# An order of its own for each engine in a recurrence over pairs of heads, with the loop written out

## The chip, the cores and the metric

The kernel runs on one core of a Trainium2 chip. The time is the device time of one execution in microseconds (us); three runs were timed. One further execution was recorded by the hardware profiler. The engines are named as in its rows: PE is the matmul engine (PEld its weight loads, PEq its instruction sequencer), DVE the vector engine, ACT the activation engine, POOL and SP the two that issue most transfers here.

## The reference, cut to what matters

A prompt of 256 tokens and 8 decode sequences of 4 tokens go through two layers of width 2048. The first layer's mixer is RWKV-7: projections r, k, v, a decay w, a rate a, and for each of 32 heads of size 64 a state matrix S that is stepped over the tokens:

```
def _wkv_step(S, inp):
    r_t, w_t, k_t, v_t, a_t, b_t = inp
    Sa = jnp.einsum('bhvk,bhk->bhv', S, a_t)
    S = S * w_t[:, :, None, :] + Sa[..., None] * b_t[:, :, None, :] + v_t[..., None] * k_t[:, :, None, :]
    y = jnp.einsum('bhvk,bhk->bhv', S, r_t)
    return S, y
...
S_last, ys = lax.scan(_wkv_step, wkv_prev.astype(f32), xs)
...
y = ((y - ym) * lax.rsqrt(yv + GN_EPS)).reshape(B, T, D) * gn_g.astype(f32) + gn_b.astype(f32)
bonus = jnp.sum(r_h * k_h * r_k.astype(f32), axis=-1, keepdims=True) * v_h
y = (y + bonus.reshape(B, T, D)).astype(x.dtype)
out = (y * g) @ w_o
```

After it come DeepNorm layer norms, SwiGLU feed-forward layers and, in the second layer, a pooling mixer. Outputs are the new tokens and the new states.

## The kernel before

All activations lie in SBUF with features on the partitions and the 288 tokens along the free axis. Every dense product is three matmuls on two halves of each operand (high times high, high times low, low times high): ACT makes the high half of a weight slab, DVE the low half, PE multiplies. The engines run their own instruction streams, in order, and meet at semaphores; `Steps` gives each engine a counter for each pair, and `await_step` waits for a named step.

The change lies in the stage of the recurrence, between the projections r, w, a, g and the product with `rw_g2`. It works on pairs of heads (128 rows): 16 pairs `p`, of which the even ones use the tiles and the three PSUM banks of `pairs[0]`, the odd ones those of `pairs[1]`. The recurrence is done in chunks of 64 tokens. The work on one pair is cut into three parts, each a Python generator whose `yield` ends a phase; each engine has its own generator, with its own instructions in the same phases:

- DENSE, phases D0 to D10: k, v and the small products for w and a of a pair. The weights come in nine pieces of 256 KB (`fetch`, three slots); PE multiplies a piece in each of D0 to D3 and D6 to D9 (D4 w, D5 a, D7 also the norm of k). DVE makes the low halves (`piece_lo`, L1607), in D9 also a reciprocal; ACT makes the high halves, in D4 k, kk and sq, in D5 the sigmoid sg, in D6 a, in D8 root, in D10 v.
- FRONT, F0 to F10: DVE's scan of the decays (L1672), csx, feats; PE turns the decode state (s0), then tok, prod (F3), two (F4), and three levels of a block inverse, x0 t0 x1 t1 x2 t2 (F5 to F10). DVE answers prod with "two" and the masks (F3), each x with a masked copy, each t with a sum (L1737), t2 also with uvx (L1748). ACT copies what PE leaves in PSUM: s0t, tok (F2), two (F4), wr, qt.
- BACK, B0 to B12: the last two levels x3 t3 x4 t4 (B0 to B3), q (B4), s0c (B5), and for the chunks 1 to 3 u and s (B6 to B11), y (B12). DVE updates the decode state in B1 (L1752, L1755), makes bonv (B4), st0 (B5, L1765), u and st, and stores y (B12, L1787). ACT copies the decode state to SOS (B2), makes mv (B3), q (B4), sop (B12).

The group norm of a pair's y is done while the next pair of the same tiles is in FRONT: PE makes the mean (L747) in F0 and the variance (L750) in F1; DVE centres in F0 and does the rest in F4 (reciprocal L1637, three more operations to L1640); ACT squares in F0 and takes the root in F2. For the last pairs this is a part of its own, NORM (N0 to N4).

`weave` puts the phases of two or three parts into one order by a fixed fraction, the same on all engines: with all three, F0 D0 B0 F1 D1 B1 B2 F2 D2 B3 F3 D3 B4 F4 D4 B5 F5 D5 B6 F6 D6 B7 B8 F7 D7 B9 F8 D8 B10 F9 D9 B11 F10 D10 B12. I call one such call a weave: in it one pair is in BACK, the next in FRONT and the one after in DENSE. `turns` makes 18 of them: the first has no BACK, the second no norm yet, twelve stand in a loop of six iterations (`Fori`, L376), the thirteenth is written out behind it, one has no DENSE, and two end with NORM. On PE a wait on a loop's index needs a register, which `await_step` computes (L732).

POOL stores the decode states of a pair when SOS is there and then loads those of the next pair of the same tiles (`results`, `states`). Scans (L1672) mark the weaves in the trace: each weave but the last two begins with one.

Of the kernel before, what the change touches and what calls it, by code (L numbers as in the profile page):

```python
# [115 lines left out]
def build(nc, x_prompt, x_sample, state_wkv, state_shift, state_pool, ln_g, ln_b, rw_mu, rw_wr, rw_wk, rw_wv,  # L116
# [4 lines left out]
    with ctx:  # L121
# [78 lines left out]
        pairs = []  # L200
# [158 lines left out]
        FRONT, BACK, NORM, DENSE = 0, 1, 2, 3  # L359
        LEVELS = [range(3), range(3, 5)]  # L360
        PHASES = [11, 13, 5, 11]

        def weave(program, *parts):


            at = [((n + (0.8 if part[2] == BACK else 0.5)) / PHASES[part[2]], q) for q, part in enumerate(parts) for n in range(PHASES[part[2]])]
            running = [program(pairs[b], 2 * i + b, i, part, normed[0] if normed else None) for b, i, part, *normed in parts]
            for _, q in sorted(at):
                next(running[q])
            assert all(next(q, None) is None for q in running)  # L370

        def turns(eng, program):
            last = KC // 2 - 1
            weave(program, (0, 0, FRONT), (1, 0, DENSE))
            weave(program, (0, 0, BACK), (1, 0, FRONT), (0, 1, DENSE))
            with eng.Fori(0, last - 1) as i:  # L376
                weave(program, (1, i, BACK), (0, i + 1, FRONT, i), (1, i + 1, DENSE))
                weave(program, (0, i + 1, BACK), (1, i + 1, FRONT, i), (0, i + 2, DENSE))
            weave(program, (1, last - 1, BACK), (0, last, FRONT, last - 1), (1, last, DENSE))
            weave(program, (0, last, BACK), (1, last, FRONT, last - 1))  # L380
            weave(program, (1, last, BACK), (0, last, NORM, last))
            weave(program, (1, last, NORM, last))

        MIXED = 6 * KC

# [246 lines left out]
        def _(pe):  # L632
# [367 lines left out]

            pe.wait_ge(lhl_ready, 4)
            pe.wait_ge(out_free, 4 + len(FIRST))
            weave(pair, (0, 0, DENSE))
            pe.wait_ge(wkv_const, 16)
            turns(pe, pair)
            for z in pairs:
                pe.wait_ge(z.ndve.sem, z.ndve.value("done", KC // 2 - 1))
            pe.sem_inc(wkv_done, 1)
# [128 lines left out]
        def _(act):  # L1137
# [243 lines left out]
            act.wait_ge(wkv_const, 16)  # L1381
            act.wait_ge(xkept, 16)

            turns(act, pair)
            for z in pairs:
                act.wait_ge(z.ndve.sem, z.ndve.value("done", KC // 2 - 1))
            act.wait_ge(wkv_done, 3)
# [86 lines left out]
            for j in range(4):  # L1474
                q = SLAB["pool"] // 4 + (j + 2) // 4
                hi(q, (j + 2) % 4, SLAB["pool"] + j + 2)
                for m in range(4):
                    n = 4 * j + m
# [10 lines left out]
        def _(dve):  # L1489
# [319 lines left out]
                next(begun)  # L1809
            dve.wait_ge(wkv_const, 16)  # L1810

            turns(dve, pair)
            for z in pairs:
                dve.wait_ge(z.ndve.sem, z.ndve.value("done", KC // 2 - 1))
            dve.sem_inc(wkv_done, 1)
# [131 lines left out]
            for lv in range(4):  # L1947
                d, f = 1 << lv, 4 * lv
                a, b = lv % 2, (lv + 1) % 2
# [26 lines left out]
            for j in range(4):  # L1976
                lo(SLAB["pool"] + j + 2, (j + 2) % 4)
                for m in range(4):
                    n = 4 * j + m
# [39 lines left out]
```

## Time and profile before

| | us |
|---|---|
| three runs | 3199.43 median, 3194.06 to 3199.57 |
| profiled execution, its own time | 3202.89 |
| its span, first to last instruction | 3201.2 |
| PE busy | 2834.5 (89%) |
| DVE busy | 1587.4 (50%) |
| ACT busy | 1193.3 (37%) |
| granted PE clock, mean | 0.932 of full |

Busy time is the union of an engine's instructions. Matmuls are pipelined and their ends modelled, so a busy PE may still be at half clock; the clock column of a stretch tells. 1.00 is 2.4 GHz and 0.50 is 1.2 GHz; values between are stretches that hold both. The recurrence runs from 254.55 us (the first scan) to 1143 us.

### The profile page before, as it was taken

To read this page: it belongs to the slowest core of one execution; us is meant where nothing else is said; L and a number is where in the kernel's file an instruction comes from. 1 tells how busy PE (TensorE), PEld (TensorE's weight loads), DVE (VectorE), ACT (ScalarE), POOL (GpSimd) and SP (SyncE) were. 2 spreads that over 40 slices of the span, in tenths; PEclk is the share of its full clock that TensorE was granted. 3 is DMA by queue.
4 is the path that set the end of the run, shared out by engine and by line. 5 is a ranking of instruction groups with operands and counts; after the bars stand their busy time and mean duration, and the time that the engine had idled before them with its cause. 6 is when DMAs were issued, how large, how long until landed. Compare 5 with 4: busy or idle time off the path is not lost.

```text
span 3201.2 us, 61665 instructions
## 1 busy us (share of the span) xinstructions
PE 2834.5 (89%) x24731; PEld 2669.6 (83%) x24731; DVE 1587.4 (50%) x2341; ACT 1193.3 (37%) x1618; POOL 170.9 (5%) x247
## 2 busy tenths in 40 slices
PE   5868888888888859899999999995699999999997
PEld 4867767667777649799999999994699999999996
DVE  5565655556555444544444444446544444444444
ACT  4344433333333122444423333334444423333333
POOL 0000010110101001000000000002100000000001
PEclk9888998889989779899999999997799999999998
DMA  6422121111212046356556565452255546665452
GB/s 189 116 54 74 54 53 53 47 54 50 53 48 56 9 138 169 98 165 170 149 145 182 166 167 161 135 169 81 66 162 166 166 135 170 174 168 166 134 162 66
DMA packets 703974, 379.37 MB, mean 119 GB/s; under 512 B 15159, under 2 KB 696487, under 8 KB 703383
## 3 DMA queue, kind: packets, MB, share of 16 engines
q1 hardware_dynamic: 697632, 361.35, 40.3%
q0 software_dynamic: 6128, 15.45, 2.0%
q8 instruction: 122, 2.00, 0.3%
q10 hardware_dynamic: 70, 0.39, 0.0%
q14 instruction: 22, 0.18, 0.0%
HBM read 367.33 MB, written 10.62 MB: 118 GB/s over the span
## 4 chain that ended last, share of the span: by engine, by line
PE 80%; DVE 11%; issue 3%; ACT 3%; DMA 1%; POOL 1%; PEld 1%; DVEq 1%; SPq 0%; PEldq 0%; ACTq 0%; POOLq 0%
PE PS L635 22%; PE PS L636 22%; PE PS L637 21%; PE PS L812 4%; DVE WL L1493 2%; ACT WH L1142 1%; PE PS L1030 1%; PE PS L864 1%; DVE TM L1637 1%; PE PS L900 1%; DVE PL L1607 1%; DVE ML L1507 1%; DVE TM L1501 1%; PE PS L836 1%; PE PS L936 1%
## 5 line engine op out<-in xcount | busy, mean ns | idle before, releaser
L1493 DVE TENSOR_TENSOR WL<-RAW,WH 128x2048 fp32r<-128x2048 f32 (+1 forms) x346 | 706.4, 2043 | 888.1 <-ACT WH L1142 888.0
L635 PE MATMUL PS<-MH,WH 128*128 128x288 f32 x3456 | 1028.6, 298 | 97.7 <-DVE ML L1507 36.3
L636 PE MATMUL PS<-ML,WH 128*128 128x288 f32 x3456 | 1031.8, 299 | 0.0
L637 PE MATMUL PS<-MH,WL 128*128 128x288 f32 x3456 | 1030.6, 298 | 0.0
L1142 ACT ACTIVATE WH<-RAW 128x2048 fp32r<-128x2048 f32 (+1 forms) x346 | 593.2, 1715 | 969.3 <-PE PS L637 947.8
L635 PEld LDWEIGHTS PS<-MH,WH 128*128 128x128 f32 x3456 | 661.3, 191 | 101.9 <-issue 71.4
L636 PEld LDWEIGHTS PS<-ML,WH 128*128 128x128 f32 x3456 | 660.9, 191 | 0.0
L637 PEld LDWEIGHTS PS<-MH,WL 128*128 128x128 f32 x3456 | 659.9, 191 | 0.0
L635 PE MATMUL PS<-HH,WH 128*128 128x288 f32 x1408 | 417.3, 296 | 16.4 <-DVEq L1893 16.4
L636 PE MATMUL PS<-HL,WH 128*128 128x288 f32 x1408 | 419.0, 298 | 0.0
L637 PE MATMUL PS<-HH,WL 128*128 128x288 f32 x1408 | 418.5, 297 | 0.0
L635 PEld LDWEIGHTS PS<-HH,WH 128*128 128x128 f32 x1408 | 268.4, 191 | 17.3 <-DVEq L1893 17.3
L636 PEld LDWEIGHTS PS<-HL,WH 128*128 128x128 f32 x1408 | 268.3, 191 | 0.0
L637 PEld LDWEIGHTS PS<-HH,WL 128*128 128x128 f32 x1408 | 268.0, 190 | 0.0
L635 PE MATMUL PS<-MH,PH 128*128 128x288 f32 x512 | 183.4, 358 | 12.9 <-DVE PL L1607 12.9
L636 PE MATMUL PS<-ML,PH 128*128 128x288 f32 x512 | 167.1, 326 | 0.0
L637 PE MATMUL PS<-MH,PL 128*128 128x288 f32 x512 | 165.6, 324 | 0.0
L1607 DVE TENSOR_TENSOR PL<-PR,PH 128x512 fp32r<-128x512 f32 x144 | 94.6, 657 | 126.0 <-ACT PH L1230 123.9
L635 PEld LDWEIGHTS PS<-MH,PH 128*128 128x128 f32 x512 | 112.0, 219 | 24.2 <-issue 12.9
L1436 ACT ACTIVATE HH<-TM 128x288 f32 (+1 forms) x88 | 39.1, 445 | 234.2 <-DVE TM L1890 234.2
L636 PEld LDWEIGHTS PS<-ML,PH 128*128 128x128 f32 x512 | 112.5, 220 | 0.7
L637 PEld LDWEIGHTS PS<-MH,PL 128*128 128x128 f32 x512 | 111.7, 218 | 0.0
(268 smaller groups left out, 2926.4 us busy)
## 6 DMA issues: line engine op xcount, KB each, us to landing
RAW<-in_ffn_w_in SPq DMA_DIRECT2D x176, 1024.0 KB, 5.7
RAW<-in_ffn_w_down SPq DMA_DIRECT2D x128, 704.0 KB, 4.7
RAW<-in_rw_wr SPq DMA_DIRECT2D x16, 1024.0 KB, 5.9
PR<-in_rw_wk SPq DMA_DIRECT2D x64, 256.0 KB, 2.8
PR<-in_rw_wv SPq DMA_DIRECT2D x64, 256.0 KB, 2.8
RAW<-in_rw_wo SPq DMA_DIRECT2D x16, 1024.0 KB, 6.0
RAW<-in_rw_g SPq DMA_DIRECT2D x4, 1024.0 KB, 5.9
S0N<-in_state_wkv POOLq DMA_DIRECT2D x64, 64.0 KB, 2.5
```

The lines of the kernel that those rows point to most:

```text
L635: pe.matmul(out, wh, xh, start=first, stop=False)
L636: pe.matmul(out, wh, xl, start=False, stop=False)
L637: return pe.matmul(out, wl, xh, start=False, stop=last)
L812: ins = pe.matmul(bank[hr[r], col + u * CH:col + (u + 1) * CH], lhs(hr[r], u), rhs(hr[r], u), start=True, stop=True)
L836: pe.transpose((PA, PB)[t][:, n * P:(n + 1) * P], f[:, t * P:(t + 1) * P], IDN)
L864: ins = pe.matmul(bank[:, t * 256:(t + 1) * 256], z.KF[hr[h], t * P:(t + 1) * P], z.AR[hr[h], :, t * P:(t + 1) * P], start=True, stop=True)
L900: ins = pe.matmul(PA[hr[h], 320 + b * 8:320 + (b + 1) * 8], z.S0T[hr[h], b, :], z.WR[hr[h], b, :], start=True, stop=True)
L936: ins = pe.matmul(PC[:, 256 + u * HN:256 + (u + 1) * HN], z.MR[:, t, h, 0:P], z.TOK[:, t, 3, hr[h]], start=True, stop=True)
L1142: act.activation(WH[0:rows, j % 2, 0:n], RAW[0:rows, j, 0:n], ACT.Copy).then_inc(hi_ready, 1)
L1436: act.activation(HH[:, bass.ds(hc, 1), :].rearrange("p a t -> p (a t)"), TM[:, b, :], ACT.Copy).then_inc(hh_ready, 1)
L1493: dve.tensor_tensor(WL[0:rows, j % 2, 0:n], RAW[0:rows, j, 0:n], WH[0:rows, j % 2, 0:n].bitcast(F32), ALU.subtract).then_inc(lo_ready, 1)
L1607: dve.tensor_tensor(PL[slot][0:rows, 0:n], PR[slot][0:rows, 0:n], PH[slot][0:rows, 0:n].bitcast(F32), ALU.subtract).then_inc(pc_lo, 1)
```

## The change

`weave` takes the engine's name and reads a string of letters, one for each engine, in which F, B and D stand for the next phase of FRONT, BACK and DENSE; letters of a part that a weave doesn't have are passed over. Weaves with NORM have one order for all engines. `turns` no longer uses the device loop: Python writes out every weave, with constants in place of registers. Which operations there are, and their operands, stays the same.

```diff
-        def weave(program, *parts):
-            at = [((n + (0.8 if part[2] == BACK else 0.5)) / PHASES[part[2]], q) for q, part in enumerate(parts) for n in range(PHASES[part[2]])]
-            running = [program(pairs[b], 2 * i + b, i, part, normed[0] if normed else None) for b, i, part, *normed in parts]
-            for _, q in sorted(at):
-                next(running[q])
-            assert all(next(q, None) is None for q in running)
-
-        def turns(eng, program):
+        ORDER = {"pe": "FDBDFBFDBFDBFDDFBDBFBDBFBFBDBFBDBDF", "dve": "FBFDFDBDBDFBDFFBDBFBBDFBDBDFBDFDBBF",
+                 "act": "FBFBDDFDDFDBBFDBDFBFBDBDFBFBFDDFBBB"}
+
+        def weave(name, program, *parts):
+            running = {"FBND"[part]: program(pairs[b], 2 * i + b, i, part, normed[0] if normed else None)
+                       for b, i, part, *normed in parts}
+            order = ORDER[name] if NORM not in [part for _, _, part, *_ in parts] else "BNBBNBBNBBNBBBNBBB"
+            for letter in order:
+                if letter in running:
+                    next(running[letter])
+            assert all(next(rest, None) is None for rest in running.values())
+
+        def turns(name, program):
             last = KC // 2 - 1
-            weave(program, (0, 0, FRONT), (1, 0, DENSE))
-            weave(program, (0, 0, BACK), (1, 0, FRONT), (0, 1, DENSE))
-            with eng.Fori(0, last - 1) as i:
-                weave(program, (1, i, BACK), (0, i + 1, FRONT, i), (1, i + 1, DENSE))
-                weave(program, (0, i + 1, BACK), (1, i + 1, FRONT, i), (0, i + 2, DENSE))
-            weave(program, (1, last - 1, BACK), (0, last, FRONT, last - 1), (1, last, DENSE))
-            weave(program, (0, last, BACK), (1, last, FRONT, last - 1))
-            weave(program, (1, last, BACK), (0, last, NORM, last))
-            weave(program, (1, last, NORM, last))
+            weave(name, program, (0, 0, FRONT), (1, 0, DENSE))
+            weave(name, program, (0, 0, BACK), (1, 0, FRONT), (0, 1, DENSE))
+            for i in range(last):
+                weave(name, program, (1, i, BACK), (0, i + 1, FRONT, i), (1, i + 1, DENSE))
+                weave(name, program, (0, i + 1, BACK), (1, i + 1, FRONT, i), *[(0, i + 2, DENSE)] * (i + 1 < last))
+            weave(name, program, (1, last, BACK), (0, last, NORM, last))
+            weave(name, program, (1, last, NORM, last))
...
-            weave(pair, (0, 0, DENSE))
+            weave("pe", pair, (0, 0, DENSE))
...
-            turns(pe, pair)
+            turns("pe", pair)
...
-            turns(act, pair)
+            turns("act", pair)
...
-            turns(dve, pair)
+            turns("dve", pair)
```

Read as phases, a full weave is now:

- PE: F0 D0 B0 D1 F1 B1 F2 D2 B2 F3 D3 B3 F4 D4 D5 F5 B4 D6 B5 F6 B6 D7 B7 F7 B8 F8 B9 D8 B10 F9 B11 D9 B12 D10 F10
- DVE: F0 B0 F1 D0 F2 D1 B1 D2 B2 D3 F3 B3 D4 F4 F5 B4 D5 B5 F6 B6 B7 D6 F7 B8 D7 B9 D8 F8 B10 D9 F9 D10 B11 B12 F10
- ACT: F0 B0 F1 B1 D0 D1 F2 D2 D3 F3 D4 B2 B3 F4 D5 B4 D6 F5 B5 F6 B6 D7 B7 D8 F7 B8 F8 B9 F9 D9 D10 F10 B10 B11 B12

## Rows read from the trace of the kernel before

**Rows 1.** The page, engines: busy us (share of the span) and instructions.
```profile
PE 2834.5 (89%) x24731; PEld 2669.6 (83%) x24731; DVE 1587.4 (50%) x2341; ACT 1193.3 (37%) x1618; POOL 170.9 (5%) x247
```
**Rows 2.** Windows by stage: length, busy (count) PE PEld DVE ACT POOL, clock, DMA.
```profile
254.55:298.07 43.52, 35.70 (x401) 30.81 (x400) 20.99 (x49) 17.18 (x35) 0.00 (x0) 0.84 0.19 53
298.07:344.53 46.46, 40.84 (x592) 33.73 (x591) 27.76 (x71) 17.92 (x41) 5.58 (x9) 0.96 0.22 60
344.53:1011.06 666.53, 562.56 (x7332) 467.99 (x7332) 375.84 (x890) 245.40 (x540) 67.01 (x108) 0.90 0.19 51
1011.06:1063.61 52.55, 46.03 (x611) 38.51 (x611) 29.87 (x73) 19.36 (x43) 5.59 (x9) 0.90 0.13 32
1063.61:1106.90 43.29, 36.50 (x525) 28.61 (x527) 23.31 (x64) 9.07 (x26) 3.13 (x5) 0.77 0.05 9
```
**Rows 3.** Waits of PE in the loop: who, for whom, us, times, longest.
```profile
PE PS L974 <- DVE ST L1765: 40.6, 12, 3.4
PE PS L747 <- issue: 24.2, 5, 5.2
PE PS L747 <- DVE R L1787: 15.2, 7, 2.2
PE PS L812 <- DVE TT L1737: 10.6, 12, 0.9
PE PS L910 <- DVE UVX L1755: 7.7, 12, 0.6
```
**Rows 4.** Windows within one weave: length, PE busy (count), clock, DMA share, GB/s.
```profile
844.69:848.94 4.25, 4.25 (x19) 0.61 0.05 10
848.94:871.95 23.01, 21.48 (x299) 1.00 0.24 61
...
875.33:882.66 7.33, 7.11 (x69) 0.54 0.25 74
882.66:896.83 14.17, 14.17 (x227) 1.00 0.15 45
```
**Rows 5.** The loop's line: sequencer, operation, count, ns least/median/most, first and last.
```profile
L376 PEldq COMPARE_BRANCH x6: 83/4643/4888, 449.2 to 1009.1; - x6
...
L376 ACTq COMPARE_BRANCH x6: 40/45/50, 449.4 to 1009.3; - x6
...
L376 DVEq COMPARE_BRANCH x6: 50/56/74, 450.3 to 1010.2; - x6
```
**Rows 6.** Timeline of DVE, three scans: start, us, line, operation, tiles.
```profile
844.34 0.75 DVE L1672 TENSOR_TENSOR_SCAN CS<-CW,SG 128x288 f32<-128x288 f32 x1
...
898.65 0.75 DVE L1672 TENSOR_TENSOR_SCAN CS<-CW,SG 128x288 f32<-128x288 f32 x1
...
956.63 0.75 DVE L1672 TENSOR_TENSOR_SCAN CS<-CW,SG 128x288 f32<-128x288 f32 x1
```
**Rows 7.** All waits of PE in the second weave, 298.07 to 344.53.
```profile
PE PS L812 <- DVE TT L1737: 1.5, 1, 1.5
PE PS L812 <- DVE XL L1728: 1.2, 2, 0.9
PE PS L974 <- DVE ST L1765: 0.7, 1, 0.7
PE PS L910 <- DVE UVX L1755: 0.4, 1, 0.4
```
**Rows 8.** Timeline of DVE: the norm's reciprocal and st0 of one weave.
```profile
870.84 1.94 DVE L1637 RECIPROCAL TM<-TM 128x288 f32<-128x288 f32 x1
...
874.91 0.28 DVE L1765 TENSOR_SCALAR ST<-PS,PC 128x64 f32<-128x64 f32 x1
```
**Rows 9.** Timeline of PE: a piece's first matmul, and what follows its twelve.
```profile
884.48 0.40 PE L635 MATMUL PS<-MH,PH 128*128 128x288 f32 x1
...
886.18 0.65 PE L793 MATMUL PS<-TM,CP 128*128 128x288 f32 x2
```
**Rows 10.** Window in the second weave, columns as in rows 2.
```profile
306.00:311.00 5.00, 4.72 (x47) 4.45 (x48) 0.65 (x2) 2.00 (x5) 1.91 (x4) 0.73 0.26 57
```

## The prediction

> **What bounds the kernel now.** I read the page first: TensorE is busy 89% of the span and carries the chain that ended last [rows 1]. That says little of a change that touches one stage only, so I cut the span into the stretches of the recurrence [rows 2]. The change reaches the first five of them: first weave, second weave, the loop of twelve, the thirteenth weave after the loop, and the one without DENSE. The loop is the prize: 666.53 us, 55.5 per weave. In it PE is busy 562.56 us, so it stands idle 103.97 us, and its mean clock is 0.90 of full.
>
> The list of PE's waits in the loop [rows 3] says what ends the idle time. Five kinds make 98.3 of the 104 us: st0 (40.6, once a weave), the back edge of the loop (24.2, five times), the last store of y before the group norm's mean (15.2), t3 before x4 (10.6), the update of the decode state (7.7). None names a DMA or ACT.
>
> One weave cut at its longest waits [rows 4] shows the second loss. After the wait at its start PE runs at half clock (0.61 over 4.25 us), then at full clock for 23.01 us with 21.48 busy, then stands for 3.38 us until 875.33 [rows 3, 4], then runs at half clock again (0.54 over 7.33 us), then full for 14.17 us. So a wait is paid twice: once as idle, once as matmuls at 1.2 GHz instead of 2.4. What the same work needs at full clock: a clock of 0.61 means that about 78% of the 4.25 us was at half speed, so 4.25 - 0.39 x 4.25 = 2.6; likewise 7.11 - 0.46 x 7.33 = 3.7; with 21.5 and 14.2 that is **42.0 us of PE work a weave** (an estimate from these rows). The loop gives the same from another side: clock 0.90 is 20% of the time, 133 us, at half speed, of which some 12 idle; half of the other 121 is excess, and (562.56 - 61)/12 = 41.8. So of 55.5 us a weave, 42 are work, 8.7 idle and about 5 low clock. DVE is busy 375.84/12 = 31.3 and ACT 20.5 us a weave: they bound nothing if their queues stand in the right order.
>
> **The change, part by part.** No instruction on tiles and no DMA is added or removed; the order within each queue is, and the loop's branches and register arithmetic go.
>
> *The back edge.* On PE the branch takes up to 4.9 us, median 4.6; on ACT 45 ns and on DVE 56 ns [rows 5]. Weaves behind it are longer: from scan to scan 54.31 us without, 57.98 with [rows 6], so 3.7 us for each of five, 18 us, and if the order did nothing else the loop would give that back. What replaces it is code executed once. The second weave was written out before too, and its waits name no fetch at all [rows 7]: I price straight code at nothing; the bound on the other side is a rival below. The Trainium skill ("Advanced Engine Details and Errata", Control Flow Timing) gives a compare-and-branch about 108 ns; by it six back edges would be worth 0.6 us. ACT and DVE agree with it roughly, PE's 4.6 us does not, and the row decides.
>
> *st0.* Before, DVE takes masks, bonv, the norm's last part and a piece, and only then st0 and x0. The reciprocal starts at 870.84 and st0 at 874.91 [rows 8]: 4.1 us, while PE has only short blocks left and then waits 3.38. In the new order DVE puts t4 ahead of the norm, and behind it x0, bonv, st0. PE's order between "two" and the first block that needs something from behind the norm (F6, which needs x0) is now D4 D5 F5 B4 D6 B5. From the moment masks are done that is F5, B4 and B5 plus a piece. A piece costs 1.70 us (884.48 to 886.18, [rows 9]); eight pieces are 13.6, so the other 24 F and B blocks and some small ones share 28.4 us, 1.15 each (estimate). Cover: 3 x 1.15 + 1.70 = 5.1 us; needed on DVE: t4 0.4, a piece 0.6, the norm 3.5 (4.1 less the piece), x0 with its mask 0.8, that is 5.3. So the 40.6/12 = 3.4 us become 0.2 to 0.5 with the hand-over.
>
> *yout.* PE now ends a weave with B12 D10 F10 and DVE with B12 F10: PE multiplies t2 while DVE stores y, and the mean follows directly. The 15.2 us (2.2 each) go; late next is uvx, which DVE makes before the next scan: x3 needs only t2, but the state product in B0 needs uvx. D0 (1.70 us) now stands ahead of B0 and F0 takes over 1 us, against TT, copies and uvx of about 1.8 us: covered.
>
> *t3 and the decode state.* Between B1 and B2 PE now has F2 and D2 (1.15 + 1.70). DVE has three operations for t3 and the state, some 2 us, but it has two pieces in front of them, whose high halves ACT makes only behind the norm's variance; following the queues by these durations I estimate t3 at 1.9 us after PE's product and the state 1.4 later, against 2.9 of cover: a wait of some 0.5 us stays of 0.9 + 0.6.
>
> *What queues behind a longer wait.* ACT's state copy sos comes some 6 us later, behind k, kk and sq, and POOL's stores and loads of states behind it. POOL is busy 67.01/12 = 5.6 us a weave with issuing them [rows 2]; with two landings I estimate a round at 10 to 11 us, so it stays hidden: sos at about 21 us leaves twice that before the next weave asks. The pieces' fetches ride on DVE's low halves as before, and in my walk each lands over 1 us before it is asked for. D5 needs ACT's sq and D6 its sg; in ACT's order both stand ahead of q, by my walk 3 and 1 us before PE asks.
>
> *The sum.* The same walk through one weave, queue by queue, leaves PE some 0.8 to 1 us idle; I double that for what I cannot see and add 0.5 for clock: 42.0 + 2.5 = **44.5 us a weave**. Loop: 666.5 - 12 x 44.5 = 132.5. Thirteenth: 52.55 - 44.5 = 8.0. Second weave (no norm in it; 46.46 now, PE 40.84 busy, about 1.7 of that low clock): 39.1 + 2.5 = 41.6, so 4.9. First (43.52; it waits on a chain with no BACK beside it): 1. The one without DENSE (43.29, clock 0.77): DVE and PE still alternate, I take 4 of at most 10 (36.50 less 5 to 7 for the clock is 30 of work, and the chain needs more). Norm weaves: nearly the order they had, 0. Sum 150.4. The profiled execution took 3202.89 us (span 3201.2), 3.5 above the median 3199.43; 3202.9 - 150 = 3053, and I keep it.
>
> **The rivals.**
> 1. *Gain as above*, a weave of 43.5 to 46.5: 13 weaves move by -13 to +26, 3040 to 3079.
> 2. *The waits get many and short, and the clock falls.* In the second weave three waits of 0.9, 1.5 and 0.4 us in a row [rows 7] were enough for a clock of 0.73 in the 5 us after 306 [rows 10]. If one such group stays in each weave, it costs 2.8 idle and, as behind st0, 3.4 of low clock: 50.7 a weave, 13 x 6.2 = 81 more, 3134; in half of the weaves, 3093. For it: hand-overs in my walk have a margin of only 0.1 to 0.9 us. Against it: the 1.53 us idle between 848.94 and 871.95 left the clock at 1.00 [rows 4]. The Trainium skill ("TensorE: Matmul & The Clock Gate", A second HAM failure mode) describes just this, short idles between groups of matmuls that let the clock swing; the two clocks here bear it out as far as rows go.
> 3. *The order does nothing*, since each engine still waits for the same partner, and only the back edge goes: 3202.9 - 18 = 3185. Against: the five waits have named partners that the new orders move.
> 4. *Slower: PE's code.* The twelve weaves are now code that PE meets once. If refills of the size of its back edge, 4.6 us, came in the middle of straight code, each weave could bear 11/4.6, a little over two, before the gain is gone; three a weave would give 3202.9 + 13 x 2.3 = 3233. Against: no wait of the straight second weave is a fetch [rows 7], and the thirteenth, straight too, is the shortest with a norm (52.55).
> 5. *Nearly no idle left*, 42.5 a weave: 3027 to 3040.
>
> **How the numbers follow.** Chances: rival 1 0.62, 2 0.24, 3 0.05, 4 0.04, 5 0.05. The predicted time is that of the first, 3053. Range 3030 to 3115: it leaves out the upper third of case 2 (0.08), 3, 4 and a little of 5, about 0.19; the first case's own range is 3040 to 3079. A change under 0.2% (6.4 us) is about what cannot be told from none. Faster is 1, 2, 3 and 5, less a little for 3: 0.95; within: 0.01; slower: 0.04.
>
> **What would show it.** Right: scans 43.5 to 46.5 us apart in the loop; PE's waits for st0 under 0.5 us each and none before the mean; the branches on line 376 gone; clock 0.97 or more over the twelve weaves; PE busy down to about 43 a weave for the same matmuls, ACT and DVE busy as before. Wrong: waits named x0, x1 or t1 of over 1 us each with a clock under 0.95 (rival 2); PE idle put down to issue in the middle of a weave (4); POOL's loads of states or a fetched piece as releaser, which I hold to be hidden.

## The result, and the profile after

The changed kernel takes 3017.44 us (median, 3010.76 to 3018.76), the kernel before 3199.09 beside it: a ratio of 0.943, 95% interval 0.941 to 0.945. The forecast of 3053 had the sign and the mechanism; its gain of 150 us was too small by 34 (184.8 between the two profiled executions), and 3017 lies below its range of 3030 to 3115.

The page of the changed kernel, engines, answers to [rows 1] (the profiled execution took 3018.05 us, its span 3016.5):

```profile
PE 2763.0 (92%) x24731; PEld 2612.4 (87%) x24731; DVE 1579.4 (52%) x2341; ACT 1190.6 (39%) x1618; POOL 170.6 (6%) x247
```

The instructions are as many as before, DVE and ACT are as busy as before, and PE is busy 71.5 us less with the same matmuls: that part of the gain is clock. The windows by stage, cut at the scans as in [rows 2] (length, busy and count of PE, PEld, DVE, ACT, POOL, clock, DMA); the last row holds all that comes after the thirteenth weave up to the end of the last group norm:

```profile
254.53:292.88 38.35, 31.76 (x398) 27.54 (x397) 20.99 (x48) 17.39 (x35) 0.00 (x0) 0.91 0.20 59
292.88:334.12 41.24, 41.01 (x607) 34.35 (x606) 27.38 (x70) 17.95 (x41) 5.58 (x9) 1.00 0.26 69
334.12:839.96 505.84, 504.73 (x7334) 421.78 (x7333) 369.08 (x889) 243.18 (x540) 66.87 (x108) 1.00 0.25 67
839.96:882.11 42.15, 42.06 (x623) 34.84 (x621) 29.55 (x73) 19.11 (x43) 5.58 (x9) 1.00 0.16 40
...
882.11:958.85 76.74, 56.32 (x700) 40.43 (x700) 38.03 (x96) 13.54 (x39) 6.24 (x10) 0.68 0.12 36
```

The row of before for that last stretch, which [rows 2] shows only in part:

```profile
1063.61:1142.84 79.23, 59.97 (x722) 42.90 (x722) 38.12 (x96) 13.67 (x39) 6.26 (x10) 0.67 0.12 36
```

Stage by stage against [rows 2]: the twelve weaves of the loop 666.53 to 505.84 (160.7), the thirteenth 52.55 to 42.15 (10.4), the second 46.46 to 41.24 (5.2), the first 43.52 to 38.35 (5.2), the rest 79.23 to 76.74 (2.5). That is 184.0 of the 184.8 us between the two profiled executions. In the loop the 160.7 have two sources: PE's idle time fell from 103.97 to 1.11 us (102.9), and its busy time, for the same matmuls, from 562.56 to 504.73 (57.8), because the clock rose from 0.90 to 1.00.

Each of the thirteen weaves with a norm is now 42.14 to 42.16 us long. The list of PE's waits over the twelve weaves is empty, where [rows 3] had five kinds of 98.3 us together; it leaves out what is as short as the 0.09 us found below. The same list for all engines, same stretch, has others at its head, and one line on PE's weight loads:

```profile
POOL out L551 <- ACT MV L1341: 227.1, 12, 19.2
...
ACT V L1278 <- PE PS L640: 49.2, 12, 4.1
...
PEld PS L815 <- DVE XL L1731: 4.0, 12, 0.3
```

At the head the others wait for PE, or for one who waits for PE: the reverse of before. The last line is the exception: once a weave the weight load of a block on x0 (tile XL, made by DVE) stands until DVE has made it. This is the place of the old st0 wait. DVE's timeline in the weave from 713.52 us (start, duration), from the masks to st0:

```profile
731.61 0.69 DVE L1712 TENSOR_TENSOR MR<-PS,CW 128x512 f32<-128x512 f32 x1 [2.16 <-PE PS L867]
732.22 0.41 DVE L1743 TENSOR_TENSOR TT<-PS,TT 128x256 f32<-128x256 f32 x1
732.55 0.68 DVE L1610 TENSOR_TENSOR PL<-PR,PH 128x512 fp32r<-128x512 f32 x1
733.15 1.95 DVE L1640 RECIPROCAL TM<-TM 128x288 f32<-128x288 f32 x1
...
736.46 0.37 DVE L1725 TENSOR_TENSOR SXL<-PS,CW 32x32 f32<-32x32 f32 x2
736.85 0.42 DVE L1731 TENSOR_TENSOR XL<-PS,CW 128x256 f32<-128x256 f32 x1
...
737.55 0.28 DVE L1768 TENSOR_SCALAR ST<-PS,PC 128x64 f32<-128x64 f32 x1
```

And PE's, same weave, at the end of B5 and in F6:

```profile
736.80 0.44 PE L970 MATMUL PS<-MR,TOK 128*64 128x128 f32 x4
737.33 0.68 PE L815 MATMUL PS<-XL,TT 64*64 64x64 f32 x16
```

The masks are done at 732.30, x0 (XL) at 737.27: DVE needs 4.97 us. PE's other work ends at 737.24, 4.94 us after the masks, and its block on x0 starts at 737.33. So PE stands 0.09 us here, in every weave with a norm, and in the twelve this is all of its idle time (12 of 0.09 are the 1.11). The 0.06 us from the end of x0 to PE's start are not slack but the hand-over from DVE to PE: e8 below, where PE stands 0.90 us for x0, has them too. st0 follows at 737.83 and is wanted 0.76 us later, at 738.59.

### The profile page after: what moved, and what is told of

Its sections match the earlier page's. It is cut to its first block, busy times and chain, and to the rows that moved or that the text cites. A ratio compares the mean times of both kernels' runs of the same rounds, so it can differ in the third digit from the quotient of the medians.

```text
span 3016.5 us, 59922 instructions
## 1 busy us (share of the span) xinstructions
PE 2763.0 (92%) x24731; PEld 2612.4 (87%) x24731; DVE 1579.4 (52%) x2341; ACT 1190.6 (39%) x1618; POOL 170.6 (6%) x247
## 4 chain that ended last, share of the span: by engine, by line
PE 83%; DVE 9%; ACT 3%; issue 2%; DMA 1%; POOL 1%; PEld 1%; SPq 0%; DVEq 0%; PEldq 0%; ACTq 0%; POOLq 0%
PE PS L638 23%; PE PS L639 23%; PE PS L640 22%; PE PS L815 4%; DVE WL L1496 2%; PE PS L1033 1%; ACT WH L1145 1%; PE PS L867 1%; DVE TM L1640 1%; PE PS L903 1%; PE PS L839 1%; DVE ML L1510 1%; PE PS L939 1%; DVE TM L1504 0%; DMA X<-x_keep 0%
## 5 line engine op out<-in xcount | busy, mean ns | idle before, releaser
L638 PE MATMUL PS<-MH,PH 128*128 128x288 f32 x512 | 169.2, 330 | 13.9 <-DVE PL L1610 13.1
L639 PE MATMUL PS<-ML,PH 128*128 128x288 f32 x512 | 154.8, 302 | 0.0
L640 PE MATMUL PS<-MH,PL 128*128 128x288 f32 x512 | 153.9, 301 | 0.0
L638 PEld LDWEIGHTS PS<-MH,PH 128*128 128x128 f32 x512 | 99.6, 194 | 37.9 <-issue 26.1
L639 PEld LDWEIGHTS PS<-ML,PH 128*128 128x128 f32 x512 | 99.8, 195 | 0.8
L640 PEld LDWEIGHTS PS<-MH,PL 128*128 128x128 f32 x512 | 99.7, 195 | 0.0
```

Of the source, the lines that this page charges most:

```text
L638: pe.matmul(out, wh, xh, start=first, stop=False)
L639: pe.matmul(out, wh, xl, start=False, stop=False)
L640: return pe.matmul(out, wl, xh, start=False, stop=last)
```

## The experiments

The kernel before took 3197.7 to 3206.9 us beside these runs; e12 and e13 have four runs each, the others one. Weaves are told from scan to scan. In diffs the lines are those of the changed kernel unless said, and `...` marks lines left out.

**e1: the loop written out, the order as it was.**

```diff
+        ORDER = {"pe": "FDBFDBBFDBFDBFDBFDBFDBBFDBFDBFDBFDB", "dve": "FDBFDBBFDBFDBFDBFDBFDBBFDBFDBFDBFDB",
+                 "act": "FDBFDBBFDBFDBFDBFDBFDBBFDBFDBFDBFDB"}
...
```

(the weaves with NORM get their old order too).

> The loop is written out, every engine keeps the one old order. Theory A (the order makes the gain, by taking PE's waits and the half clock behind them away): only the back edge goes, 3.7 us for each of five or six, so 18 to 22 us less than before, 3177 to 3185 us; the waits for st0 (3.4 us) and for the last store of y (2.2 us) stay in every weave. Rival B (the loop, with its branch and its register arithmetic, was the loss): most of the 182 us come already here, under 3110 us.

It took 3153.74 us, 50 less than before: neither number. The weaves are 51.2 to 53.3 long. Over the twelve (window, then PE's waits: total, times, longest):

```profile
344.43:964.37 619.94, 540.79 (x7332) 0.93 0.21 55
```

```profile
PE PS L977 <- DVE ST L1768: 37.5, 12, 3.1
PE PS L750 <- DVE R L1790: 23.6, 12, 2.0
```

The old waits are there; the one for the last store of y, named 7 times in [rows 3], comes 12 times now that no back edge hides it. In these twelve weaves idle time fell by 103.97 - 79.15 = 24.8 us, about the 24.2 of the back edges [rows 3]; PE's busy time fell by another 21.8 us, which is low clock. The forecast had priced a back edge by the difference of two weaves, one behind an edge and one not [rows 6]. That misses that without the edges the clock is better in both kinds: one stretch at half clock in most weaves, where all but one of the twelve had two.

**e2: the orders of the change, kept inside the device loop.**

```diff
-            for i in range(last):
+            with eng.Fori(0, last - 1) as i:
...
```

(the last iteration stands behind the loop, as in the kernel before).

> The new orders, with the device loop of six iterations kept. Theory A: weaves inside an iteration at 42.2 us; at the back edge PE has no wait left in which the 4.6 us could hide, and half clock may follow, so 4.6 to 8 us for each of five or six, 3040 to 3065 us. Rival B: the loop was the loss, over 3110 us.

It took 3050.74 us. Two weaves of one iteration, the first one behind a back edge, and the two largest entries of PE's waits in the twelve:

```profile
692.50:742.03 49.53, 46.43 (x623) 0.93 0.22 58
742.03:784.43 42.40, 40.32 (x601) 1.00 0.26 67
```

```profile
PE PS L752 <- issue: 22.1, 5, 4.7
PE PS L817 <- DVE XL L1733: 3.2, 12, 0.3
```

The orders alone are worth 153 us. A back edge costs 4.4 us idle and makes its weave 7.1 longer, the rest being half clock behind it. The Trainium skill ("Advanced Engine Details and Errata", Control Flow Timing) gives a compare-and-branch about 108 ns. This row of PE says forty times as much; ACT's 45 and DVE's 56 ns [rows 5] are about half of it, where the prediction had them agree roughly. The twelve weaves grow by 544.44 - 505.84 = 38.6 us: five edges of 7.1, and 0.25 a weave for x0, for which PE now stands up to 0.35 us instead of 0.09 (from the end of x0 to PE's start it is 0.15 us in this loop, 0.06 in straight code). So the two parts are 153 and 50 alone and 182 together. In the twelve weaves they are 122.1 (666.53 - 544.44), 46.6 and 160.7: 8 us could be had by either. They are low clock, since writing the loop out takes 21.8 us off PE's busy time under the old order and 11.8 under the new (516.57 in e2 to 504.73). The rest of the overlap lies outside these weaves and isn't explained; single runs differ there by several us.

**e3, e5, e10, e11: whose order matters.** In each, some engines take another's order. Four kernels; the strings are PE's new one, P, and the old common one, O:

```diff
 e3:  "pe": P, "dve": P, "act": P
 e5:  "pe": P, "dve": O, "act": its own
 e10: "pe": P, "dve": P, "act": its own
 e11: "pe": P, "dve": its own, "act": P
```

> PE's new order given to DVE and ACT too, loop written out. Theory A1 (the hand-overs are tight, so each engine's own order counts): weaves of 43 to 46 us with new waits of PE, 3030 to 3070 us. Rival (only PE's order counts, since DVE is busy 70 and ACT 45 per cent of a weave): 3012 to 3024 us, no difference from the change.

> PE and ACT in their new orders, DVE in the old common one, loop written out. Theory A1: DVE's order is tight; x0 and st0 stand behind other phases again and PE waits, with half clock behind the longer waits, 47 to 53 us a weave, 3080 to 3160 us. Rival (DVE has slack): 3012 to 3030 us.

> DVE takes PE's order of phases, ACT keeps its own. With PE's order for all three the run took 3073 us and PE waited for two things in a weave: sq from ACT (1.4 us) and feats from DVE (0.8 us). Theory A (each wait belongs to the one engine that is named): only the wait for feats comes back, 0.8 us a weave, 42.9 to 43.3 us from scan to scan, 3027 to 3037. Rival B (the orders hang together, DVE's alone is worth as much as all three): 3050 or more, with a clock under 0.98.

> ACT takes PE's order of phases, DVE keeps its own: the counterpart of the run in which DVE alone took PE's order (3091 us, waits for x blocks that no sum of the single waits gave). Theory A (ACT's order matters through sq alone, PE's wait of 1.4 us in D5): 43.5 to 45.5 us from scan to scan, 3040 to 3065. Rival B (what one engine's order costs can't be told from the waits of the run with all three alike): waits under other names than sq, and a time outside 3040 to 3065.

They took 3073.18, 3330.13, 3091.47 and 3104.55 us. The twelve weaves and PE's waits in them, e3 first:

```profile
343.38:894.30 550.92, 524.48 (x7334) 0.97 0.23 62
```

```profile
PE PS L638 <- ACT TM L1265: 16.5, 12, 1.4
PE PS L839 <- DVE KF L1693: 9.1, 12, 0.8
```

e10, DVE alone in PE's order:

```profile
340.41:914.06 573.65, 531.42 (x7334) 0.95 0.22 59
```

```profile
PE PS L815 <- DVE XL L1731: 33.0, 24, 2.1
PE PS L839 <- DVE KF L1693: 8.0, 12, 1.0
```

e11, ACT alone in PE's order:

```profile
348.67:922.80 574.13, 541.89 (x7334) 0.93 0.21 59
```

```profile
PE PS L638 <- ACT TM L1265: 16.5, 12, 1.4
PE PS L815 <- DVE TT L1740: 15.8, 12, 1.3
```

e5, DVE in the old order:

```profile
347.81:1121.11 773.30, 617.38 (x7332) 0.83 0.17 44
```

```profile
PE PS L815 <- DVE XL L1731: 73.9, 31, 4.0
PE PS L815 <- DVE STT L1708: 35.4, 12, 3.0
PE PS L750 <- DVE R L1790: 29.1, 12, 2.4
```

In e3 an order of its own for each engine is worth 45 us in the loop over one good order for all: two waits, for sq and for feats, and some low clock. But these two waits don't belong to ACT and DVE one by one. With only DVE in PE's order the wait for feats comes back as expected (0.7 us), and with it a new one for x blocks, twice a weave and up to 2.1 us, that e3 didn't have; with only ACT in it, sq comes back and a wait for a t block of 1.3. Rival B was right in both: two engines in step and the third in another order is worse than all three in step. e5 is the far end: PE's new order with DVE in the old one is 127 us slower than the kernel before. The change for the worse was expected, but less than half of it, and not a kernel slower than before: 13 us idle a weave, and 9.4 of low clock.

The old order for PE alone, or for ACT alone, wasn't tried. For ACT alone the queues would wait for each other in a circle: the old ACT puts q ahead of sq, while the new PE puts D5, which wants sq, ahead of B4, which makes q.

**e8, e9, e14: what a later x0 costs.** One DVE operation more in each weave, whose result nobody reads: 0.9 us ahead of x0 (e8), the same behind the update of the decode state (e9), 2.6 us ahead of x0 (e14).

```diff
                     norm("rest")
+                    dve.reciprocal(z.ST[:, :, :].rearrange("p a b -> p (a b)"), z.PC[:, 0:P])
                     yield
```

> Gives DVE one more operation of about 0.9 us (a reciprocal of 128x128 whose result nobody reads) right ahead of its x0, where the trace of the changed kernel shows a margin of 0.06 us (x0 done 737.27, PE's F6 starts 737.33). Theory A (the chain of the norm and x0 is the tightest hand-over, with no slack): PE waits 0.8 to 0.9 us in every weave with a norm, the weave grows to 43 us and the run to 3027 to 3032, more if the clock falls too. Rival B (PE's blocks ahead of F6 are not pinned to DVE, there is slack that the trace hides): the run stays at 3014 to 3021 and PE shows no wait.

> The same extra DVE operation of about 0.9 us, now right behind the update of the decode state in B1, where DVE stands idle for some 1.9 us in each weave of the changed kernel. Theory A (what counts is the margin of a hand-over, not DVE's busy time): nothing moves, 3012 to 3022. Rival B (DVE's busy time is what the weave pays for): as much as ahead of x0, 3027 to 3032.

> As the run with 0.9 us more ahead of x0, but with one reciprocal of 384 columns (288 take 1.95 us, so some 2.6), result unused: PE's wait ahead of F6 grows to about 2.5 us in each of the 13 weaves with a norm. Theory A (a lone wait costs itself and no more, as 0.9 us did): 44.7 us from scan to scan at full clock, 3049 to 3053. Rival B (a wait of this length takes the clock down behind it, as the prediction's second rival priced it: 3.4 us more): 46 to 48.2 us, a clock of 0.93 or less, 3065 to 3096.

They took 3027.40, 3025.18 and 3074.28 us. e8, the twelve weaves and PE's waits:

```profile
335.72:851.23 515.51, 504.72 (x7334) 1.00 0.25 66
```

```profile
PE PS L815 <- DVE XL L1732: 10.8, 12, 0.9
```

One weave of e8, x0 on DVE and the block on PE that wants it:

```profile
746.49 0.42 DVE L1732 TENSOR_TENSOR XL<-PS,CW 128x256 f32<-128x256 f32 x1
...
746.97 0.68 PE L815 MATMUL PS<-XL,TT 64*64 64x64 f32 x16 [0.90 <-DVE XL L1732]
```

e8 is theory A to the letter: 0.81 us a weave, 42.95, at full clock. x0 ends at 746.91 and PE, which has stood 0.90 us for it, starts 0.06 later, as in the changed kernel. So the margin of 0.06 us, of which the expectation speaks, is the time of the hand-over: PE's wait grows from 0.09 to 0.90 and the weave by the same 0.81, and there was no slack at this place at all. e9, the twelve weaves and the rest up to the last norm:

```profile
334.16:839.97 505.81, 504.70 (x7334) 1.00 0.25 67
...
882.12:964.50 82.38, 62.16 (x700) 45.04 (x700) 39.63 (x98) 13.55 (x39) 6.26 (x10) 0.61 0.11 34
```

The same operation in the other place costs the twelve weaves nothing (505.81 against 505.84), as theory A had it. The run is nevertheless 8 us longer, outside what A gave: 5.6 of it stand in the tail (82.38 against 76.74), where PE has no DENSE to cover DVE and the clock fell from 0.68 to 0.61. e14, two neighbouring weaves and the wait in both:

```profile
747.59:793.58 45.99, 43.49 (x613) 0.96 0.23 62
793.58:838.13 44.55, 42.05 (x613) 1.00 0.23 63
```

```profile
PE PS L815 <- DVE XL L1732: 5.0, 2, 2.5
```

Same wait, same work, one weave at full clock throughout and one not. In 11 of the 13 weaves the wait of 2.5 us was followed by a stretch of 3.4 us at half clock and cost 1.5 more; in two it cost itself alone. Rival B was right that the clock falls, and the run lies in its range, but its price of 3.4 was over twice what is measured.

**e7: less PE work.** Leaves out one of three matmuls of every dense product in the recurrence (weight high times activation low).

```diff
-                            ins = three(bank[:, 0:T], PH[slot][:, k * P:(k + 1) * P], PL[slot][:, k * P:(k + 1) * P],
-                                        xh[:, k0 + k, :], xl[:, k0 + k, :], k0 + k == 0, k0 + k == KC - 1)
+                            pe.matmul(bank[:, 0:T], PH[slot][:, wk], xh[:, k0 + k, :], start=k0 + k == 0, stop=False)
+                            ins = pe.matmul(bank[:, 0:T], PL[slot][:, wk], xh[:, k0 + k, :], start=False,
+                                            stop=k0 + k == KC - 1)
...
```

> Leaves out one of the three matmuls of every dense product in the recurrence (weight high times activation low), 32 matmuls or about 4.2 us of PE work in a weave. Theory A (after the change PE's own work sets the weave, 42.1 us of 42.15, and every other queue has slack, though little at some hand-overs): the weave falls by most of what PE loses, to 38 to 39.5 us, and the run to 2955 to 2985. Rival B (the chain over DVE and ACT is as long as PE's queue already, so that PE's work was only just covered): the weave stays at 41 us or more, PE shows waits of 3 us and more in each, and the run stays over 3005.

It took 2997.53 us, between the two. One weave at full clock, and PE's waits in the twelve; then, from another weave, PE's last wait and a stretch at half clock (all engines):

```profile
658.60:698.23 39.63, 38.26 (x581) 1.00 0.27 72
```

```profile
PE PS L817 <- DVE XL L1733: 10.6, 23, 0.6
PE PS L841 <- DVE KF L1695: 4.6, 11, 0.4
```

```profile
355.05 0.68 PE L817 MATMUL PS<-XL,TT 64*64 64x64 f32 x16 [0.63 <-DVE XL L1733]
...
367.47:370.88 3.41, 3.41 (x29) 2.85 (x30) 1.79 (x7) 1.18 (x3) 0.00 (x0) 0.50 0.05 15
```

PE lost 3.8 us of work a weave. In the weaves at full clock 2.5 of them arrive, 1.3 come back as waits. In nine of the twelve the clock falls for a stretch as well, and eight of these take 40.9 us. No wait here is longer than 0.63 us, less than in e8, and in the weave shown the stretch begins 12 us behind the last of them, with PE busy all the time between: it can't be put down to one wait, and its cause is open. So the other queues have some slack behind PE, but little.

**e12, e13: the tail.** After 882 us PE still runs at a mean clock of 0.68. e12 moves the norm's phases forward in the one weave of BACK with NORM; e13 does that too and gives PE matmuls whose results nobody reads, four in place of each missing DENSE phase and 40 behind the recurrence.

```diff
-            order = ORDER[name] if NORM not in [part for _, _, part, *_ in parts] else "BNBBNBBNBBNBBBNBBB"
+            order = ORDER[name] if NORM not in [part for _, _, part, *_ in parts] else "BNBNNBNBNBBBBBBBBB"
```

```diff
+            def keep_busy(n):
+                pe.wait_ge(pairs[1].dact.sem, pairs[1].dact.value("v", KC // 2 - 1))
+                for k in range(n):
+                    pe.matmul(D0[:, 0:T], PH[0][:, 0:P], MH[1][:, k % KC, :], start=True, stop=True)
...
```

> Only the weave of BACK with NORM changes its order, the same on all engines: the norm's phases come early, so that its reciprocal no longer stands ahead of u for the last chunk, for which PE waits 3.2 us near 948 us in the changed kernel. Theory A (that wait is the price of the reciprocal): 2 to 4 us less in the tail, 3013 to 3016. Rival B (PE and DVE alternate there anyway and the wait comes back under another name): the same time, 3016 to 3019.

> The early norm, and PE gets matmuls whose results nobody reads where the weaves without DENSE leave it idle: four at each place where a DENSE phase would stand, and 40 behind the recurrence while the product that follows waits for its operands. In the changed kernel the tail from 882 us to the end of the last norm takes 76.7 us at a mean clock of 0.68. Theory A (half clock is a good part of the tail's length): the clock there rises over 0.85 and the run falls to 2998 to 3010. Rival B (PE waits in a chain with DVE, whose lengths the clock hardly touches, and the added matmuls stand in its way): 3014 or more.

e12 took 3013.96 us (ratio to before 0.942, interval 0.941 to 0.944), e13 3010.96 (0.942, 0.940 to 0.943). The tail, cut as in the windows of the result, in e12 and then in e13:

```profile
881.87:954.24 72.37, 54.91 (x700) 39.17 (x700) 37.90 (x96) 13.65 (x39) 6.24 (x10) 0.72 0.13 38
```

```profile
881.71:948.18 66.47, 61.07 (x846) 48.40 (x845) 37.63 (x96) 13.66 (x39) 6.24 (x10) 1.00 0.15 42
```

In the traces the tail falls from 76.74 to 72.37 and 66.47, the latter at full clock with more matmuls: theory A in both, as far as the tail goes. The whole run falls less, and e13's 3010.96 lies just above what A gave: from the end of the last norm to the end of the span it is 2057.6 us in the changed kernel, 2058.5 in e12 and 2061.2 in e13. Over kernels of this study that don't touch that stretch it is 2053.6 (e8) to 2060.6 (e7), so whether e13 gives anything back there can't be told. Both medians are below that of the change, by 3.5 and 6.5 us; the intervals overlap, and neither step is settled as a gain over the change.

## Why the prediction was off

*Work and bound: right.* The estimate of 42.0 us of PE work a weave measured 42.06, in all thirteen. PE at full clock became the bound, together with DVE's chain up to x0, which is just as long (e8).

*The five waits: right, and more so.* Four went whole, and of the one at st0 0.09 us are left, for x0. The forecast left 0.2 to 0.5 us ahead of F6 and 0.5 in B2. For F6 PE's cover was estimated at 5.1 and measured at 4.94; DVE's need was put at 5.3 and is 5.03 with the hand-over, since the norm took 3.3 instead of 3.5 and t4 overlaps its neighbours. For B2, in the same weave, PE's t3 and the two blocks that follow the piece, then DVE's t3 and its last operation on the state:

```profile
718.69 0.63 PE L815 MATMUL PS<-TT,XL 64*64 64x64 f32 x16
...
722.67 0.68 PE L815 MATMUL PS<-TT,LT 64*64 64x64 f32 x16
723.28 0.66 PE L913 MATMUL PS<-CP,UVX 128*128 128x128 f32 x4
```

```profile
720.46 0.68 DVE L1740 TENSOR_TENSOR TT<-PS,TT 128x512 f32<-128x512 f32 x1
...
721.77 0.69 DVE L1758 TENSOR_TENSOR UVX<-UVX,PC 128x512 f32<-128x512 f32 x1
```

PE's product for t3 ends at 719.32. DVE has t3 done 1.8 us later (estimated at 1.9), at 721.14, and PE wants it at 722.67: 1.5 us to spare. The state is done 3.1 us behind the product (estimated at 3.3), at 722.46, and PE wants it only at 723.28: 0.8 to spare. The cover was put at 2.9 and is 3.35 (F2 is 1.6 us long, not 1.15), and the forecast held the state against it as well, though PE multiplies x4 (0.6 us) before it wants the state. So the need was about right in both places; what was missed is cover in B2.

*The allowance: the step that failed.* "I double that for what I cannot see and add 0.5 for clock: 42.0 + 2.5". What remains beside the work is 0.09 us, and no low clock at all. The weave is 2.35 us shorter than the 44.5 of the sum, in each of 13 weaves: 30.6 of the 34 us that the forecast missed. Of the 2.5, 1.5 were the doubling and the clock, for which the runs show nothing; the other 1 was the walk's own idle time, of which 0.09 came. The clock was no independent allowance here: with 0.09 us of waiting a weave it stayed at 1.00, and e8 shows that a lone 0.9 us leaves it there too. That waits alone set it is not shown (e7).

*The first weave.* Put at 1, it gave 5.2: PE's idle time fell by 1.2 only (7.82 to 6.59), its busy time by 3.9, clock 0.84 to 0.91. The forecast looked at the chain and not at its clock. The second weave gave 5.2 for 4.9; the tail 2.5 for 4.

*The back edge.* Priced at 3.7 each and 18 in all, it is 7.1 each with the new orders (e2) and 50 us in all with the old one (e1): the idle part was read about right (24.2 in [rows 3], 24.8 in e1), the low clock left out. In the sum this was hidden, since the weaves were priced as a whole. It sat openly in rival 3, whose 3185 would have been 3154.

*The rivals.* Rival 5 came nearest and had 0.05; it was close to the walk's own result (0.8 to 1 us idle) without the doubling, and deserved more. Even its 3027 was too high, by the first weave and by the last 0.3 us of each other. Rival 2's mechanism exists: in e14 a wait of 2.5 us takes the clock down in most weaves. The Trainium skill ("TensorE: Matmul & The Clock Gate", A second HAM failure mode) has frequent short idles between groups of matmuls swing the clock. e7 fits it in part, with three waits of 0.28 to 0.63 us in a weave and half clock in nine of the twelve, though not right behind a wait; the lone waits of e8 and e14 are another case. The changed kernel never came there: its one wait is 0.09 us. Rival 4 is out: PE meets all twelve weaves once and has no wait for issue in them. (Its sum has a slip: three refills of 4.6 less 11 are 2.8 a weave and not 2.3, so 3239 and not 3233.) What the forecast held to be hidden (POOL's states, the pieces' fetches, ACT's sq and sg) was hidden.

What stays open: why the same wait takes the clock down in eleven weaves of e14 and not in two, what takes it down in e7, and whether e12 and e13 are gains over the change.

## What to carry to other kernels

When engines run in order and meet at semaphores, one order for all need not be the best that the same work allows (here 45 us behind in the loop, e3), but the orders are one object: change one engine's and the waits move to places that no single wait foretold. Walk the queues by the durations of the trace, and then believe the walk: an allowance for the unseen, multiplied by the number of repeats, was here most of the error. And before a small gap between a maker's end and a user's start is called slack, compare it with the same gap where the user is known to wait. A wait on the matmul engine can cost twice, as idle and as low clock behind it; where the waits of a stretch went, the second price went with them.

## What the runs showed of the hardware that was not expected

- A loop's back edge costs PE 4.4 us of standing and makes the weave behind it 7.1 us longer (e2); DVE and ACT pass theirs in some 50 ns [rows 5].
- One and the same wait of 2.5 us was followed by half clock in 11 weaves and not in two (e14); a lone wait of 0.9 us never was in 13 (e8), and yet a weave with three waits of at most 0.63 us had half clock in nine cases of twelve (e7).
- From the end of DVE's operation to the start of the PE block that stood for it 0.06 us pass, whether PE stood 0.09 us (the changed kernel) or 0.90 (e8).
- Matmuls whose results nobody reads, put where PE would stand, took the tail's clock from 0.72 to 1.00 and shortened it by 5.9 us, though PE did more (e13 against e12).
